# A two-layer streaming encoder on one core: the MLP's tokens split 288 and 256, and one product of 512 columns for the high and low parts of the second half

## What is computed

```
def _layer(x, l, p, k_past, v_past, conv_buf, h0):
    ...
    x = x + _rms(m @ p['w_out'], p['g_mix_post'])
    f = jnp.square(jax.nn.relu(_rms(x, p['g_mlp_pre']) @ p['w_up'])) @ p['w_down']
    x = x + _rms(f, p['g_mlp_post'])
    return x, k_rows, v, conv_new, h_last
```

## Time and profile before

| what | value |
| --- | --- |
| median of 3 runs | 2021.5 us |
| lowest and highest | 2019.04, 2022.38 us |
| span of the profiled execution | 2018.6 us |
| TensorE busy in it | 98% |
| VectorE, ScalarE, GpSimd busy | 53%, 47%, 14% |

### The profile page before, as it was taken

How to read it: one execution, slowest core, us unless ns; L and a number is a source line. 1 busy time by engine, 2 the same in 40 slices (tenths; PEclk the granted TensorE clock), 3 DMA queues, 4 the chain that set the end, 5 groups by cost and what they waited for, 6 DMA issues and landing times.

```text
span 2018.6 us, 38666 instructions
## 1 busy us (share of the span) xinstructions
PE 1975.9 (98%) x15630; PEld 1929.2 (96%) x15630; DVE 1072.3 (53%) x1986; ACT 955.6 (47%) x1503; POOL 279.1 (14%) x306
## 2 busy tenths in 40 slices
PE   7999999999999999999989999999999999999997
PEld 7999999999998999999989999999999999999997
DVE  6657575765437432333467676767644464224334
ACT  5466666565236431342365757565732554213333
POOL 4312121100101200120041212120001012002100
PEclk9999999999999999999999999999999999999999
DMA  5323232322332323232323232322223323233331
GB/s 136 107 60 105 63 100 69 83 71 78 93 95 70 87 84 93 84 94 84 98 60 98 64 100 72 99 76 75 74 84 94 95 65 92 84 92 86 90 88 67
DMA packets 308455, 172.00 MB, mean 85 GB/s; under 512 B 7592, under 2 KB 303872, under 8 KB 308320
## 3 DMA queue, kind: packets, MB, share of 16 engines
q1 hardware_dynamic: 300768, 155.47, 27.0%
q0 software_dynamic: 7520, 14.59, 2.6%
q10 hardware_dynamic: 32, 0.04, 0.0%
HBM read 158.86 MB, written 11.21 MB: 84 GB/s over the span
## 4 chain that ended last, share of the span: by engine, by line
PE 81%; ACT 9%; DVE 6%; issue 3%; DMA 1%; SPq 0%; ACTq 0%; DVEq 0%
PE PJ L698 65%; PE PJ L710 3%; PE PJ L880 3%; PE PX L908 2%; ACT w_hi L1136 2%; PE PX L926 1%; DVE w_lo L1611 1%; PE PX L946 1%; DVE T L1722 1%; PE PX L962 1%; PE PX L710 1%; DMA w_raw<-in_w_in 1%; DVE uc L1855 1%; ACT L1353 1%; DVE Y L1643 1%
## 5 line engine op out<-in xcount | busy, mean ns | idle before, releaser
L1611 DVE TENSOR_TENSOR w_lo<-w_raw,w_hi 128x1024 fp32r<-128x1024 f32 x284 | 384.2, 1356 | 371.5 <-ACT w_hi L1136 370.4
L698 PE MATMUL PJ<-h_hi,w_hi 128*128 128x272 f32 x2304 | 489.9, 294 | 2.6 <-DVE T L1722 1.9
L698 PE MATMUL PJ<-h_hi,w_lo 128*128 128x272 f32 x2304 | 474.8, 288 | 0.0
L698 PE MATMUL PJ<-h_lo,w_hi 128*128 128x272 f32 x2304 | 473.8, 287 | 0.0
L1136 ACT ACTIVATE w_hi<-w_raw 128x1024 fp32r<-128x1024 f32 x284 | 297.6, 1051 | 233.4 <-DMA w_raw<-in_w_down 116.9
L698 PEld LDWEIGHTS PJ<-h_hi,w_hi 128*128 128x128 f32 x2304 | 359.3, 189 | 12.8 <-issue 9.5
L698 PEld LDWEIGHTS PJ<-h_lo,w_hi 128*128 128x128 f32 x2304 | 360.7, 188 | 0.0
L698 PEld LDWEIGHTS PJ<-h_hi,w_lo 128*128 128x128 f32 x2304 | 359.5, 189 | 0.0
L698 PE MATMUL PJ<-u_hi,w_hi 128*128 128x272 f32 x960 | 198.4, 288 | 0.0
L698 PE MATMUL PJ<-u_hi,w_lo 128*128 128x272 f32 x960 | 197.4, 288 | 0.0
L698 PE MATMUL PJ<-u_lo,w_hi 128*128 128x272 f32 x960 | 197.1, 287 | 0.0
(11 more groups left out here) (351 smaller groups left out, 3595.4 us busy)
## 6 DMA issues: line engine op xcount, KB each, us to landing
w_raw<-in_w_in SPq DMA_DIRECT2D x110, 512.0 KB, 3.8
w_raw<-in_w_down SPq DMA_DIRECT2D x64, 512.0 KB, 3.8
w_raw<-in_w_up SPq DMA_DIRECT2D x62, 512.0 KB, 4.1
w_raw<-in_w_branch_attn SPq DMA_DIRECT2D x16, 512.0 KB, 3.8
w_raw<-in_w_branch_lru SPq DMA_DIRECT2D x16, 512.0 KB, 3.8
w_raw<-in_w_out SPq DMA_DIRECT2D x16, 512.0 KB, 3.8
out_prompt_k<-stage POOLq DMA_DIRECT2D x16, 256.0 KB, 2.8
out_prompt_v<-GA POOLq DMA_DIRECT2D x8, 512.0 KB, 4.5
```

The lines of the kernel that those rows point to most:

```text
L698: mm = pe.matmul(PJ[:, buf, half, 0:HT], w[a], src[b][:, k0 + k, HT * half:HT * half + HT], start=first and k == 0 and a + b == 0, stop=en ...
L1611: dve.tensor_tensor(low(n)[:], raw(n), w_hi[:, n.hi, :, :].bitcast(F32), ALU.subtract).then_inc(w_lo_ready, 1)
```

## The change

For the up and down tiles that went through `gemm`, and for the first two tiles in `down_end`, TensorE now runs `parts_gemm`. The tokens of a tile are split 288 and 256. The first half is done as before in three products of 288 columns, added up in the bank `PJ[:, buf, 0]`. For the second half, the high and the low part of the activations are put side by side (`h_both`, `u_both` are the same memory as before, seen as one tensor), and one product of 512 columns multiplies both by the high part of the weights; its two sums of 256 columns lie side by side in the bank `PJ[:, buf, 1]`. The product of the low weights with the high part adds to the second of them. So a k block has five products: 288, 256, 288, 512 and 288 columns.

VectorE adds the two sums when it empties the bank. For an up tile it takes max(x, 0) of the first half, copies one sum of the second half to `T`, adds the other, and takes max(x, 0) of that in place, with waits on its own semaphore `parts_added` between. For a down pair of c = 0 it copies one sum and the first half and then adds the other sum (`f_begun`); for c = 1 it adds first one sum, the first half, then the other (`f_added`).

```diff
-        h_hi = at("h_hi", [P, KT, NT], F32R, H_AT)
-        h_lo = at("h_lo", [P, KT, NT], F32R, H_AT + KT * TILE)
+        h_both = at("h_both", [P, 2, KT, NT], F32R, H_AT)
+        h_hi, h_lo = h_both[:, 0], h_both[:, 1]
...
-        u_hi = at("u_hi", [P, 16, NT], F32R, BIG)
-        u_lo = at("u_lo", [P, 16, NT], F32R, BIG + 16 * TILE)
+        u_both = at("u_both", [P, 2, 16, NT], F32R, BIG)
+        u_hi, u_lo = u_both[:, 0], u_both[:, 1]
...
+            def parts_gemm(n, src, k0, buf, free, first=True, end=True, waits=None):
+
+                hi, lo, both = src
+                tile_in(n)
+                need(pe, evacuated, free)
+                o, both_o = PJ[:, buf, 0, 0:HW[0]], PJ[:, buf, 1, :].rearrange("p (a c) -> p a c", a=2)
+                for k in range(KT):
+                    if waits is not None:
+                        pe.wait_ge(waits[0], waits[1] + k)
+                    begin, last_k = first and k == 0, end and k == KT - 1
+                    wh, wl = w_hi[:, n.hi, k, :], low(n)[:, k, :]
+                    pe.matmul(o, wh, hi[:, k0 + k, HC[0]], start=begin, stop=False)
+                    if k > 0:
+                        pe.matmul(both_o[:, 1, :], wl, hi[:, k0 + k, HC[1]], start=False, stop=False, skip_group_check=True)
+                    pe.matmul(o, wh, lo[:, k0 + k, HC[0]], start=False, stop=False)
+                    pe.matmul(both_o, wh, both[:, :, k0 + k, HC[1]], start=begin, stop=last_k, skip_group_check=True)
+                    if k == 0:
+                        pe.matmul(both_o[:, 1, :], wl, hi[:, k0 + k, HC[1]], start=False, stop=False, skip_group_check=True)
+                    mm = pe.matmul(o, wl, hi[:, k0 + k, HC[0]], start=False, stop=last_k)
+                    if k == KT - 1:
+                        mm.then_inc(tile_done, 1)
...
-                    gemm(n, H, 0, j % 2, n.value - 2 if isinstance(r, int) and j == 0 else n.value - 1)
+                    parts_gemm(n, (h_hi, h_lo, h_both), 0, j % 2, n.value - 2 if isinstance(r, int) and j == 0 else n.value - 1)
...
-                    gemm(n, (u_hi, u_lo), 8 * half, j // 2, (n.value - 1 if fresh else n.value - 2) if half == 0 else 0,
+                    parts_gemm(n, (u_hi, u_lo, u_both), 8 * half, j // 2, (n.value - 1 if fresh else n.value - 2) if half == 0 else 0,
...
-                    gemm(n, U_, 8 * half, 0, n.value - 2 if half == 0 else 0, first=half == 0, end=half == 1)
+                    parts_gemm(n, (u_hi, u_lo, u_both), 8 * half, 0, n.value - 2 if half == 0 else 0, first=half == 0, end=half == 1)
...
-                            dve.tensor_scalar(halves(T[:, j % 2, :]), proj(n), 0.0, None, ALU.max).then_inc(evacuated, 1)
+                            dve.tensor_scalar(T[:, j % 2, HC[0]], PJ[:, j % 2, 0, 0:HW[0]], 0.0, None, ALU.max)
+                            dve.tensor_copy(T[:, j % 2, HC[1]], PJ[:, j % 2, 1, HW[1]:]).then_inc(parts_added, 1)
+                            dve.wait_ge(parts_added, 2 * (28 * l + 16 * c + 4 * r + j - 4) + 1)
+                            dve.tensor_tensor(T[:, j % 2, HC[1]], T[:, j % 2, HC[1]], PJ[:, j % 2, 1, 0:HW[1]], ALU.add).then_inc(parts_added, 1)
+                            dve.wait_ge(parts_added, 2 * (28 * l + 16 * c + 4 * r + j - 4) + 2)
+                            dve.tensor_scalar(T[:, j % 2, HC[1]], T[:, j % 2, HC[1]], 0.0, None, ALU.max).then_inc(evacuated, 1)
...
-                for half in range(2):
-                    cl = slice(HT * half, HT * half + HT)
-                    dve.tensor_tensor(Y[:, m, cl], Y[:, m, cl], PJ[:, m % 2, half, 0:HT], ALU.add).then_inc(evacuated, 1)
+                dve.tensor_tensor(Y[:, m, HC[1]], Y[:, m, HC[1]], PJ[:, m % 2, 1, 0:HW[1]], ALU.add).then_inc(f_added, 1)
+                dve.tensor_tensor(Y[:, m, HC[0]], Y[:, m, HC[0]], PJ[:, m % 2, 0, 0:HW[0]], ALU.add).then_inc(evacuated, 1)
+                dve.wait_ge(f_added, 7 * l + m + 1)
+                dve.tensor_tensor(Y[:, m, HC[1]], Y[:, m, HC[1]], PJ[:, m % 2, 1, HW[1]:], ALU.add).then_inc(evacuated, 1)
...
+                        dve.tensor_copy(Y[:, m, HC[1]], PJ[:, j, 1, 0:HW[1]]).then_inc(f_begun, 1)
+                        dve.tensor_copy(Y[:, m, HC[0]], PJ[:, j, 0, 0:HW[0]]).then_inc(evacuated, 1)
+                        dve.wait_ge(f_begun, 8 * l + 2 * r + j + 1)
+                        dve.tensor_tensor(Y[:, m, HC[1]], Y[:, m, HC[1]], PJ[:, j, 1, HW[1]:], ALU.add).then_inc(evacuated, 1)
```

More of the change, by code:

```diff
@@ L252, in hybrid_encoder @@
         f_gained, half_trio = sem("f_gained"), sem("half_trio")
+        parts_added, f_begun, f_added = map(sem, ("parts_added", "f_begun", "f_added"))
         out_turned, last_turned, last_placed, out_stored = map(sem, ("out_turned", "last_turned", "last_placed", "out_stored"))
@@ L1934, in down_four @@
                         dve.wait_ge(tile_done, n.value + 2)
[L1935 to L1939, removed]
+                        if not isinstance(r, int):
+                            own_wait(dve)
+                        dve.tensor_copy(Y[:, m, HC[1]], PJ[:, j, 1, 0:HW[1]]).then_inc(f_begun, 1)
+                        dve.tensor_copy(Y[:, m, HC[0]], PJ[:, j, 0, 0:HW[0]]).then_inc(evacuated, 1)
+                        dve.wait_ge(f_begun, 8 * l + 2 * r + j + 1)
+                        dve.tensor_tensor(Y[:, m, HC[1]], Y[:, m, HC[1]], PJ[:, j, 1, HW[1]:], ALU.add).then_inc(evacuated, 1)
                     else:
```

## The result

The changed kernel takes 2026.16 us (median of 18 runs, 2023.98 to 2027.98), the kernel before 2021.16 (18 runs). The ratio is 1.0019, 95% interval 1.0012 to 1.0026: some 4 us slower, about the 0.2% that a measurement can tell. The forecast was 2018.0 us, 3.5 us the other way; the median is 1.2 us above the upper end of its range (2025 us). The profiled execution has a span of 2023.8 us, 5.2 more than before.

A forecast was written before the change was run, and what follows sets the result against it. The prediction took TensorE, busy for 98% of the span, as the bound, through its price per product. Fewer products (-3.7 us) and VectorE's thin margin (+0.2) gave -3.5 us: 2021.5 to 2018.0 us, range 2013 to 2025.

The forecast's parts named there:

- The bound: MLP on TensorE: unbroken products at granted clock 1.00, 124.45 ns each, so only the price per product counts.
- The worth of a product fewer: Changed MLP tiles: each of 928 k steps loses one product's fixed 3.95 ns, 3.7 us in all.
- the price of the five new products by a line: Changed tiles' k step: 0.443 ns a column plus 3.95 ns a product, 742.75 ns against 746.7 before.
- The lever from 128 to 512 columns: Start distances of 0.06 us at 128 columns and 0.23 at 512 in the trace, giving 0.443 ns a column.
- The half tiles' prices: A layer's last two down tiles, already at 288 and 256 columns: 132.3 and 118.5 ns a product.
- half-tile price: Rival: the new products cost about 1 ns above the line, losing 0.9 us, 2022.4 us; chance 0.20.
- the four steps: VectorE's evacuation of an up tile: max, copy, add, max in 1.62 us, 0.91 more than before.
- the ring: Up tiles' loop of evacuation, square, `u_hi`, `split_hi`, `split_lo`: 4.84 us grows to 5.75, under a tile's 5.942.
- The 0.2 us that were charged for the thin margin: First-half up tiles: 0.2 us charged for both layers, for semaphores on a margin of 0.1.
- VectorE's ring: Rival: VectorE sets the pace in the first half's 12 up tiles, up to 2029.7 us; chance 0.10.
- The fixed price of 11.1 ns: Rival: each product costs a fixed 11.1 ns, so the kernel gains 10.3 us, 2011.2 us; chance 0.10.
- 131 ns for 512 columns: Rival: the product of 512 takes 131 ns, saving 103.8 ns a step, about 1959 us; chance 0.01.

The follow-up runs named there:

- run 2: Changed kernel with the product of 512 columns as two of 256, all else kept: 2027.62 us, 753.4 ns a step.
- run 4: Kernel before, tokens 512 to 543 left out of these products, once as three products of 512 and once as six of 256: 699.9 and 710.0 ns a step.
- run 1: Changed kernel with its five products reordered by weights, high three times then low twice (288, 512, 288, 256, 288): 2021.75 us, ratio to before 0.9995.
- run 9: Changed kernel in two other orders: 288, 288, 512, 256, 288 took 748.3 ns a step; 512, 288, 288, 288, 256 took 746.9 ns, 2021.25 us.
- run 3: Kernel before with tokens split 288 and 256, six products in its own order, no sum for VectorE: 2028.6 us, ratio 1.003.
- run 5: Kernel before with tokens split 288 and 256, the three products of 288 ahead of the three of 256: 753.3 ns a step.
- run 7: Changed kernel with an up tile's evacuation back to two maxima, the sum of the second half's low part left out: 71.99 us for 96 steps.
- run 6: Changed kernel with its sequence of widths, but weights dealt to change twice a step and not four times: 749.9 ns a step.
- run 11: Kernel before with the second half's operand begun at column 256, not 272, still six products of 272 columns: 756.5 ns a step.
- run 8: Kernel before with six products of 288 columns, the second half's operand begun at column 256, 32 columns computed twice: 795.0 ns a step.

## Why the prediction was wrong

- **The bound** was right: the MLP stays one unbroken run of products at a granted clock of 1.00, and the time is their price.
- **The worth of a product fewer** was nearly right. The fixed part was put at 3.95 ns; joining two products of 256 is worth 3.4 to 3.5 ns in runs 2 and 4. For 928 steps that is 3.2 us, where 3.7 were forecast. But it is no price of its own: in the orders of runs 1 and 9 five products cost 4.9 to 6.3 ns less than six of the same widths.
- **The step that failed is the price of the five new products by a line** (0.443 ns a column and 3.95 ns, 742.75 ns a step). It took the split for free, since the columns are the same. The split costs 6.6 ns a step, 6.2 us in both layers (run 3), nearly twice what the joint product gives back in this order. Measured are 749.9 and 750.5 ns, some 7 more. By the distances of starts in the changed kernel (the line's price first): 288 columns 131.5 and 132.5, three times a step; 256, 117.4 and 120.1; 512, 230.8 and 232.2. So 5.7 of the 7 ns lie in the products of 288 and 256, which the prediction saw 0.8 and 1.1 ns above its line and put back on it; the product of 512 stayed within the 224 to 235 ns that the prediction set for it. The lever from 128 to 512 columns was long, but its starts are read to 0.01 us: 0.17 us over 384 columns cannot tell 0.443 ns a column from 0.459.
- **The numbers for the right answer stood in the prediction.** The half tiles' prices and the upper bound of 512, 0.459 ns a column, give 3 x 132.3 + 118.5 + 235.0 = 750.4 ns. That it meets 750 so closely is luck in part: the sum is the same for every order, and two orders take 746.9. The rival *half-tile price* took the first but put 512 at only 1 ns above the line, and so ended at 747.75 ns and 2022.4 us; the range was built on that. Its sign was right. The objection against it, that the half tiles write one bank all the time, does not hold: with banks in turn or three times running the price is the same (runs 3 and 5).
- **VectorE** was right in size: 1.56 us for the four steps (1.62 forecast), 5.71 for the ring (5.75), the down pairs hidden. The 0.2 us that were charged for the thin margin were not paid (run 7). An own wait left 0.03 to 0.04 us between two instructions. So the rival *VectorE's ring* did not occur.
- **The fixed price of 11.1 ns** falls: a joined pair would have saved 11 ns, and saved 3.4 to 3.5 where only that was changed (runs 2 and 4), 6.3 at most.
- **131 ns for 512 columns** falls: a product of 512 with its weight load takes 233.3 ns in a stream of its kind (run 4). The Trainium skill ("TensorE: Matmul & The Clock Gate", section "Back-to-back issue gap") states about 131 ns for such a stream; the trace does not agree.
- **The order of the products** was not thought of at all as a price. The forecast took the sum of the columns; the four orders of the same five products lie between 746.9 and 749.9 ns. The changed kernel has the dearest of the four, and that is 3.0 of the 3.3 ns by which its step is dearer than before.

What stays open: by what rule a step's price follows from the places where its operands begin, the widths and the order. Changes of weights (runs 2, 3 and 6), unlike neighbours among six products (runs 4 and 5) and VectorE's evacuation (run 7) are ruled out. The place where the second half lies is shown to count by itself (run 11), and so is the order (runs 1 and 9). The prices of single products don't add up to a step: 3 x 132.5 + 118.3 + 233.3 = 749.1 ns would hold for all four orders. Whether the second half's place is also what makes 288/256 dear in six products was not varied by itself. The record speaks for the widths there: 256 columns cost 118.5 ns with every operand at column 288 and 118.3 at columns 0 and 256 in turn (run 4), 288 columns 132.3 ns at column 0 alone and 132.5 at 0 and 256 (run 8). At these places their prices did not move; that of 272 did. No arrangement of five products beat six of 272 by more than the measurement can tell.

## What to carry to other kernels

Where TensorE is busy without a gap, price a changed step with the widths, the operands' first columns and the order that it will have: at equal columns these moved a step here by up to 10 ns of 747, where one product fewer was worth 3.5 to 6.3. Before work is re-split to save an instruction, run the split alone with the old instruction count; here it would have shown 6.6 ns a step against the 3.95 that were hoped for. Then try the orders of what is left: here they decided whether the change lost 3.3 ns a step or next to nothing. And where a term has two bounds, add up the bounds of all terms on one side before the range is closed.

## What was not expected of the hardware

- Six products of 272 columns cost 746.6 ns when the second half's operand begins at column 272 of a row of 544, and 756.5 ns when it begins at 256 (run 11).
- The same five products cost 746.9, 748.3 or 749.9 ns a step, by their order (after, runs 1 and 9); dealing the high and low weights differently to the same sequence of widths changed nothing (run 6).
- Such a step repeats very exactly: three kernels with the same sequence of widths (after, runs 6 and 7) take 71.99 us for 96 steps, all three, and 276.20, 276.19 and 276.19 us for 368.
- With a weight load each, products of 256, 272, 288 and 512 columns cost 118.3, 124.4, 132.5 and 233.3 ns in streams of their kind. From 256 to 512 columns that is 115.0 ns more, 0.449 ns a column at a granted clock of 1.00, which leaves 3.3 ns a product that do not grow with the columns. By that line 288 would be 132.7 and 272 would be 125.5: 272 lies 1.1 ns below it with the halves at 0 and 272, and 0.6 above it at 0 and 256 (756.5 / 6 = 126.1, run 11).
